# A hybrid encoder step on one core: the later tokens' last output column tile by tile, and their norm turned before it is scaled

## The chip, the cores and the metric

The kernel runs on one core of a Trainium2 chip. The metric is the device time of one execution in microseconds (us). Engine names in rows: PE is TensorE (PEld its weight loads), DVE is VectorE, ACT ScalarE, POOL GpSimd, SP SyncE; a q behind a name is that engine's issuing of DMAs.

## What is computed

One layer for 512 prompt tokens and 128 sample tokens (8 sequences of 16), 2048 wide, all float32. Cut to what matters:

```
m = silu(c) @ w_ada + b_ada;  sh1, sc1, g1, sh2, sc2, g2 = split(m, 6)     # one row per sequence
h = rmsnorm(x, norm1_g) * (1 + sc1) + sh1
z = h @ w_in        # GLU value, GLU gate, q, k, v
y_conv = silu(layernorm(causal_dwconv(za * sigmoid(zg))));  o = band_attention(q, k, v)
x = x + g1 * (concat(y_conv, o) @ w_out)
h2 = rmsnorm(x, norm2_g) * (1 + sc2) + sh2
q = h2 @ w_pq;  s = q . sub_keys;  top 16 x top 16 -> top 16 of 16384 experts, for each of 8 heads
out = sum_e softmax(s)_e * gelu(h2 . u_e) * v_e
x = x + g2 * out;  y = rmsnorm(x, final_g)
```

The prompt tokens share one conditioning row, so their scale and shift are the same for every token; the sample's differ by sequence.

## The kernel before

Tokens lie in five tiles of 128 rows: tiles 0 to 3 are the prompt's, tile 4 is the sample's. The kernel takes tiles 0 and 1 (the first tokens, `TX` = 2) through projections, attention, output projection, norm and key queries, and then tiles 2, 3 and 4 (the later tokens, `TY` = 3) through the same. While TensorE is at the later tokens, VectorE already works on the first tokens' experts.

**Expert steps.** One `step(n)` is one expert of one token tile: POOL gathers 128 rows of `u_experts` (1 MB) into one of `NU` = 4 buffers (line 695), and VectorE multiplies them with h2 and sums (line 2009). There are 5 x 8 x 16 = 640. POOL gathers at most four steps ahead. Between steps VectorE makes the choice of the next heads' experts (`choose`). The order of VectorE's work is written out by hand: `steps(k)` puts k expert steps at a place.

**The scatter and the dense passes.** For tiles 0 to 3 the value side is dense: after step 272 (`TX * P + AHEAD`) VectorE, ScalarE and POOL make one-hot rows (`burst(0)`), TensorE scatters the weights of tiles 0 and 1 into W (line 1212), and then multiplies W with all 128 blocks of 128 rows of `v_experts` (1 MB each, line 1223). After step 512 VectorE drains the eight banks (line 1939), and the same follows for tiles 2 and 3. The sample's value side is gathered row by row at the end (line 2121). W takes the place of all that lies in RB. So ScalarE's `keep_W(0)` waits until h2 and the key scores of the later tokens are stored to DRAM (`s_h2s`, `s_Ss`, lines 1553 and 1554).

**The stretch of the change.** The later tokens' output projection has four column blocks j of 512. `w_out` comes in four quarters of 1 MB (four of the 16 row blocks each), each with one buffer that is free again when the block's three tiles have used it (`w_used`, for the fourth quarter `o_done`). The loop is block, quarter, tile (lines 1157 to 1168); a quarter of a tile is four float32 matmuls of 512 columns, each two instructions in the trace. The twelve results are numbered v = 3 j + t. VectorE multiplies each with the gate and adds it to x1 (lines 2092 and 2093, `o_free`), with `steps(4)` behind each of v = 0 to 8, then 2, 1, 1 steps behind v = 9 to 11. Beside v = 10 and 11 and behind them comes `norm_tile` for tiles 2, 3 and 4: `row_scales` (sum of the four partial sums, square root on ScalarE, reciprocal, one refinement), then x1 = x1 * r * A2 + B2 in two passes of 2048. `A2` is (1 + sc2) * norm2_g, `B2` is sh2, spread over 128 partitions; for the sample both have 16 equal rows for each sequence. The sample's B2 is loaded in eight pieces into the buffer of the prompt's gate rows, which is free after v = 10. ScalarE makes the sums of squares of a tile after its last column (`row_squares`, into banks 4 to 7), and stores the last column of x1 to DRAM. TensorE turns each h2 tile with 16 transposes into four banks (`turn_h2`), ScalarE copies them out (`keep_h2T`), and then TensorE makes key queries in 16 column blocks (lines 1177 to 1190), between them the key scores.

SP issues in this order: last `w_out` block (line 453), x1 columns 0 to 1535 of each tile after v = 6, 7, 8 (line 528), the first `w_pq` block (line 453), the sample's B2 (line 534), h2 of each tile (line 537), the other `w_pq` blocks, and at the end the key scores (lines 545 and 547).

## Time and profile before

| | us |
|---|---|
| median of 3 runs | 4024.66 |
| lowest and highest | 4020.64, 4044.64 |
| the profiled execution's own time | 4015.18 |
| its span | 4013.4 |

The rows that follow are of the profiled execution. Its own time is 1.8 us more than its span, and 9.5 us below the median of the runs. Times are counted from the start of the span. A busy time is that of the engine alone; what stands in brackets behind a row is how long the engine stood idle before it, and what ended that.

### The profile page before, as it was taken

To read this page: it belongs to the slowest core of one execution; us is meant where nothing else is said; L and a number is where in the kernel's file an instruction comes from. 1 tells how busy PE (TensorE), PEld (TensorE's weight loads), DVE (VectorE), ACT (ScalarE), POOL (GpSimd) and SP (SyncE) were. 2 spreads that over 40 slices of the span, in tenths; PEclk is the share of its full clock that TensorE was granted. 3 is DMA by queue.
4 is the path that set the end of the run, shared out by engine and by line. 5 is a ranking of instruction groups with operands and counts; after the bars stand their busy time and mean duration, and the time that the engine had idled before them with its cause. 6 is when DMAs were issued, how large, how long until landed. Compare 5 with 4: busy or idle time off the path is not lost.

```text
span 4013.4 us, 33736 instructions
## 1 busy us (share of the span) xinstructions
PE 3568.6 (89%) x11903; PEld 1887.8 (47%) x11903; DVE 2743.8 (68%) x4847; ACT 450.0 (11%) x1066; POOL 1211.2 (30%) x1052
## 2 busy tenths in 40 slices
PE   4899998997994989797889999999688999997992
PEld 1566544475542754465534444444363444443441
DVE  1258843158788968879876667776897676655577
ACT  2100004010000530103400000000070000000000
POOL 1000001116423535446542222222473222222233
PEclk8999999998996789898999999999899999998996
DMA  9877753569999999997499999999919999999997
GB/s 369 272 237 256 256 184 124 174 213 405 411 415 411 376 352 385 376 409 300 186 417 421 421 414 412 421 419 418 383 71 420 421 421 421 421 421 391 421 417 307
DMA packets 344751, 1401.89 MB, mean 349 GB/s; under 512 B 22832, under 2 KB 146952, under 8 KB 203237
## 3 DMA queue, kind: packets, MB, share of 16 engines
q0 software_dynamic: 116784, 831.78, 51.0%
q1 hardware_dynamic: 226800, 563.12, 37.4%
q10 hardware_dynamic: 1008, 4.98, 0.3%
q8 instruction: 86, 1.41, 0.1%
q14 instruction: 73, 0.60, 0.0%
HBM read 1375.08 MB, written 31.42 MB: 350 GB/s over the span
## 4 chain that ended last, share of the span: by engine, by line
DMA 49%; PE 26%; issue 12%; DVE 10%; POOL 2%; ACT 0%; SPq 0%; DVEq 0%; POOLq 0%; ACTq 0%
DMA R<-in_u_experts,MS 36%; DMA R<-in_v_experts,MS 10%; PE bank L833 8%; PE bank L861 7%; PE bank L1048 4%; DVE R L1919 3%; DMA R<-in_w_ada 3%; POOL R L695 2%; DVE R L2121 2%; PE bank L773 1%; DVE R L2009 1%; PE bank L1055 1%; PE bank L750 1%; DVE R L1918 1%; DMA keyscore_scratch<-RB 0%
## 5 line engine op out<-in xcount | busy, mean ns | idle before, releaser
L695 POOL DMA_INDIRECT R<-in_u_experts,MS x640 | 889.3, 1390 | 1564.2 <-DVE MS L2009 1321.6
L2009 DVE CUSTOM_DVE_ANT_0 R<-R 128x2048 f32<-128x2048 f32 x368 | 844.6, 2295 | 417.8 <-DMA R<-in_u_experts,MS 406.2
L1223 PE MATMUL bank<-R,RB 128*128 128x512 f32 x2304 | 1019.2, 600 | 82.4 <-DMA R<-in_v_experts 82.4
L1223 PE MATMUL bank<-RB 128*128 128x512 f32 x1792 | 778.2, 592 | 0.0
L1223 PEld LDWEIGHTS bank<-R,RB 128*128 128x128 f32 x2304 | 440.2, 192 | 651.3 <-issue 550.8
L2009 DVE CUSTOM_DVE_ANT_0 R<-R,RB 128x2048 f32<-128x2048 f32 x272 | 622.8, 2290 | 113.5 <-DMA R<-in_u_experts,MS 112.4
L1223 PEld LDWEIGHTS bank<-RB 128*128 128x128 f32 x1792 | 340.5, 190 | 428.6 <-issue 428.6
L833 PE MATMUL bank<-RB,R 128*128 128x256 f32 (+1 forms) x1536 | 399.9, 421 | 28.4 <-DMA R<-in_w_pq 25.2
L2121 DVE SCALAR_TENSOR_TENSOR R<-R,MS 128x2048 f32<-128x2048 f32 x128 | 301.4, 2355 | 180.1 <-DMA R<-in_v_experts,MS 177.7
L833 PEld LDWEIGHTS bank<-RB,R 128*128 128x128 f32 x1536 | 294.2, 193 | 127.0 <-DMA R<-in_w_pq 25.8
L1048 PE MATMUL bank<-RB,R 128*128 128x384 f32 x1024 | 333.1, 486 | 1.2 <-ACT RB L1384 0.7
L861 PE MATMUL bank<-R,RB 128*128 128x512 f32 x640 | 276.6, 594 | 0.5 <-issue 0.5
L1055 PE MATMUL bank<-R,RB 128*128 128x512 f32 x576 | 252.9, 601 | 8.2 <-DMA R<-in_w_in 7.6
L695 POOL DMA_INDIRECT R<-in_v_experts,MS x128 | 150.3, 1174 | 357.0 <-DVE R L2121 335.2
L1048 PEld LDWEIGHTS bank<-RB,R 128*128 128x128 f32 x1024 | 193.3, 190 | 133.2 <-ACT RB L1384 1.1
L861 PEld LDWEIGHTS bank<-R,RB 128*128 128x128 f32 x640 | 121.5, 191 | 151.8 <-issue 151.8
L1055 PEld LDWEIGHTS bank<-R,RB 128*128 128x128 f32 x576 | 110.7, 193 | 149.0 <-issue 137.9
L1683 DVE SCALAR_TENSOR_TENSOR RB<-RB,MS 128x512 f32<-128x512 f32 x240 | 175.9, 733 | 0.0
L1212 PE MATMUL bank<-R 128*128 128x128 f32 x1024 | 145.5, 295 | 31.4 <-DVE R L1919 19.9
L1919 DVE TENSOR_SCALAR R<-MS 128x128 f32<-128x128 f32 x512 | 150.6, 353 | 9.0 <-PE bank L1212 9.0
L1212 PEld LDWEIGHTS bank<-R 128*128 128x128 f32 x1024 | 129.0, 199 | 48.4 <-DVE R L1919 37.7
L750 PE MATMUL bank<-MS,RB 128*128 128x128 f32 (+5 forms) x497 | 75.6, 301 | 74.1 <-DMA RB<-in_rel_bias_table 16.6
(317 smaller groups left out, 2178.6 us busy)
## 6 DMA issues: line engine op xcount, KB each, us to landing
R<-in_v_experts SPq DMA_DIRECT2D x144, 1024.0 KB, 9.1
RB<-in_v_experts SPq DMA_DIRECT2D x112, 1024.0 KB, 9.1
R<-in_w_ada SPq DMA_DIRECT2D x48, 2048.0 KB, 13.4
R<-in_w_in SPq DMA_DIRECT2D x20, 2048.0 KB, 18.3
R<-in_w_in SPq DMA_DIRECT2D x24, 1024.0 KB, 25.9
R<-in_w_out SPq DMA_DIRECT2D x8, 2048.0 KB, 8.0
R<-in_w_pq SPq DMA_DIRECT2D x8, 2048.0 KB, 10.4
R<-in_w_out SPq DMA_DIRECT2D x16, 1024.0 KB, 15.8
```

Source lines behind the costliest of these rows:

```text
L695: pool.indirect_dma_start(dst, None, table, bass.IndirectOffsetOnAxis(ap=expert[T_ % 2][:, c:c + 1], axis=0)).then_inc(signal, 16)
L750: return pe.transpose(out, in_, ident[0:k, 0:k])
L833: m = pe.matmul(PB[2 * par + i][:, 0:src.shape[-1]], w, src[:, k], start=(k == 0), stop=(k == KT - 1))
L861: m = pe.matmul(PB[bank][:, :], src[:, 8 * half + i, t * P:(t + 1) * P], wide[:, slot, i, :], start=(half + i == 0), stop=(half + i == 8))
L1048: m = pe.matmul(PB[bank][:, 0:NY], quad[:, q, i, c * P:(c + 1) * P], src[:, 4 * q + i], start=(q + i == 0), stop=(q + i == 6))
L1055: m = pe.matmul(PB[bank][:, :], src[:, 4 * q + i, t * P:(t + 1) * P], quad[:, q, i, :], start=(q + i == 0), stop=(q + i == 6))
L1212: m = pe.matmul(PB[n % 4][:, k * P:(k + 1) * P], oneh[n % 4][:, 1, k], oneh[n % 4][:, 0, k], start=True, stop=True)
L1223: x = pe.matmul(PB[4 * h + q][:, :], W[:, i, h * P:(h + 1) * P], vring[slot][:, q * PW:(q + 1) * PW], start=(i == 0), stop=(i == NKEY - 1))
L1683: ch.mark(STT(out=oP, in0=iP, scalar=w, in1=oP, op0=ALU.mult, op1=ALU.add))
L1919: m = TS(oneh[n % 4][:, 0, k], iota_row, turned[t % 2][:, 0, c:c + 1], turned[t % 2][:, 2, c:c + 1], ALU.is_equal, ALU.mult)
L2009: V.tensor_tensor_reduce(u, u, x, 1.0, 0.0, ALU.mult, ALU.add, dots[t % 2][:, h * TOPK + s:h * TOPK + s + 1]).then_inc(dots_done, 1)
L2121: STT(out=acc, in0=pick_rows[p % NPICK], scalar=weight[TP][:, p:p + 1], in1=acc, op0=ALU.mult, op1=ALU.add).then_inc(v_used, 1)
```

## The change

It is made in the later tokens' stretch, and has these parts:

- The sample tile comes first in each column block (`YORDER` = sample, tile 2, tile 3), for TensorE, VectorE, ScalarE and the stores.
- In the last column block TensorE takes the four quarters of one tile, then those of the next, in place of each quarter for all three.
- The sample's B2 has the sample's own gate rows as its buffer, free after v = 9, and SP issues it ahead of the first `w_pq` block.
- ScalarE squares every result as it is added (`later_square`), into two banks and two places of RB that nothing else uses then, instead of four per tile at the end.
- Only the sample tile is normed as before the turn. The two prompt tiles are scaled by their row scale alone (`xnY`: tile 2 in place, once its x1 is stored, tile 3 into the buffer of the prompt's gate rows), turned, and get A2 and B2 as per-partition scale and bias on the way out of PSUM: tile 2 on ScalarE, tile 3 on VectorE, 16 instructions of 128 columns each. `abY` holds these two, copied once by VectorE ahead of the first tokens' choices.
- The row-wise h2 of the two prompt tiles, needed for the expert steps and the store, is made behind that.
- VectorE's order: v = 9, two steps, v = 10, wait for all of B2, sample norm, row scales and copy of tile 2, v = 11, row scales and copy of tile 3, one step, the copies out of PSUM, h2 of tiles 2 and 3, the other steps. `step` waits for all of h2 before expert step 256.

```diff
--- before.py
+++ after.py
@@ -150,12 +150,16 @@
...
         xnX = [n2X, g1X]
+        YORDER = (TY - 1, *range(TY - 1))
+        abY = RB[:, 32768:32768 + 2 * KT].rearrange("p (o k) -> p o k", o=2)
...
         A2Y = [rb(KB + (2 + i) * D, D) for i in range(2)]
-        B2Y = [rb(KB + 4 * D, D), rb(KB, D)]
+        B2Y = [rb(KB + 4 * D, D), g1Y[1]]
+        xnY = [x1[TX], g1Y[0]]
+        squares = [PB[6][:, :], PB[7][:, :], rb(30720, PW), rb(30720 + PW, PW)]
@@ -523,18 +527,18 @@
...
             def x1_out(j, cols):
-                for t in range(TX, T):
-                    sp.wait_ge(o_free, 4 + 8 + 3 * j + t - TX + 1)
-                    sp.dma_start(x1_d[t][:, cols], x1[t][:, cols]).then_inc(s_x1t[t], 16)
+                for i, y in enumerate(YORDER):
+                    sp.wait_ge(o_free, 4 + 8 + 3 * j + i + 1)
+                    sp.dma_start(x1_d[TX + y][:, cols], x1[TX + y][:, cols]).then_inc(s_x1t[TX + y], 16)
...
             x1_out(2, slice(0, 3 * PW))
-            load_block(10, "w_pq", 0)
-            sp.wait_ge(o_free, 4 + 8 + 11)
+            sp.wait_ge(o_free, 4 + 8 + 10)
...
                 sp.dma_start(B2Y[1][NS * b:NS * b + NS], rows(mod_d, [[0, NS]], D, (1 + b) * 6 * D + 3 * D)).then_inc(s_sh2, 16)
-            for t in range(TX, T):
-                sp.wait_ge(s_h2, t + 1)
-                sp.dma_start(h2_d[t], x1[t]).then_inc(s_h2s, 16)
+            load_block(10, "w_pq", 0)
+            for i, y in enumerate(YORDER):
+                sp.wait_ge(s_h2, TX + i + 1)
+                sp.dma_start(h2_d[TX + y], x1[TX + y]).then_inc(s_h2s, 16)
@@ -982,12 +986,11 @@
...
-            def turn_h2(t, x):
-                pe.wait_ge(s_h2, t + 1)
+            def turn_h2(x, bank):
...
                         k = 4 * q + i
-                        m = tr(PB[4 * (t % 2) + q][:, i * P:(i + 1) * P], x[:, k * P:(k + 1) * P], P)
+                        m = tr(PB[bank + q][:, i * P:(i + 1) * P], x[:, k * P:(k + 1) * P], P)
@@ -1154,26 +1157,37 @@
...
             pe.wait_ge(pv_read, 2 * NH)
-            for j in range(4):
+            def out_quarter(j, q, i):
+                v = j * TY + i
+                if q == 0 and v >= 6:
+                    pe.wait_ge(o_free, 4 + 8 + v - 5)
+                m = quarter_rows(catY, q, YORDER[i], (v + 3) % 6)
+                if q == 3:
+                    m.then_inc(o_done, 1)
+                elif i == TY - 1:
+                    m.then_inc(w_used, 1)
+
+            for j in range(3):
...
                     weights_in(q)
-                    for t in range(TY):
-                        v = j * TY + t
-                        if q == 0 and v >= 6:
-                            pe.wait_ge(o_free, 4 + 8 + v - 5)
-                        m = quarter_rows(catY, q, t, (v + 3) % 6)
-                        if q == 3:
-                            m.then_inc(o_done, 1)
-                        elif t == TY - 1:
-                            m.then_inc(w_used, 1)
+                    for i in range(TY):
+                        out_quarter(j, q, i)
+            for i in range(TY):
+                for q in range(4):
+                    if i == 0:
+                        weights_in(q)
+                    out_quarter(3, q, i)
+            pe.wait_ge(o_free, 4 + 8 + 9)
+            pe.wait_ge(s_h2, TX + 1)
+            turn_h2(x1[TP], 4)
             pe.wait_ge(o_free, 4 + 8 + 12)
-            for t in range(TX, T):
-                if t == TX + 1:
-                    pe.wait_ge(s_sq, 2 * T)
-                if t == TX + 2:
-                    pe.wait_ge(s_h2E, 4 * (TX + 1))
-                turn_h2(t, x1[t])
-            pe.wait_ge(s_h2E, 4 * T)
+            pe.wait_ge(s_xn, T + TX + 1)
+            turn_h2(xnY[0], 0)
+            pe.wait_ge(s_xn, T + TX + 2)
+            pe.wait_ge(s_h2E, 4 * (TX + 1))
+            turn_h2(xnY[1], 4)
+            pe.wait_ge(s_h2E, 4 * (TX + 2))
+            pe.wait_ge(xT_dve, KT + KT // 2 + 4)
@@ -1368,21 +1382,33 @@
...
-            def row_squares(t, x, ready):
-                act.wait_ge(o_free, ready)
-                for c in range(4):
-                    if t >= 1:
-                        act.wait_ge(s_sq, T + t)
-                    m = A(PB[4 + c][:, :], x[:, c * 512:(c + 1) * 512], ACT.Square, accum_out=part[:, t, c:c + 1])
-                m.then_inc(s_sq, 1)
-                act.wait_ge(s_v1, t + 2)
+            def later_square(c, i):
+                t = TX + YORDER[i]
+                act.wait_ge(o_free, 4 + 8 + 3 * c + i + 1)
+                if c == 3:
+                    act.dma_start(x1_d[t][:, 3 * PW:], x1[t][:, 3 * PW:]).then_inc(s_x1t[t], 16)
+                n = TY * c + i
+                if n >= 4:
+                    act.wait_ge(s_sq, T + TX + n - 3)
+                A(squares[n % 4], x1[t][:, c * PW:(c + 1) * PW], ACT.Square, accum_out=part[:, t, c:c + 1]).then_inc(s_sq, 1)
+
+            def later_sqrt(i):
+                t = TX + YORDER[i]
+                act.wait_ge(s_v1, TX + i + 2)
...
-            def keep_h2T(t, dst, at):
+            def keep_h2T():
                 for q in range(4):
-                    act.wait_ge(s_h2T, 4 * t + q + 1)
-                    A(dst[:, 4 * q:4 * q + 4, at * P:(at + 1) * P],
-                      PB[4 * (t % 2) + q][:, :].rearrange("p (k n) -> p k n", k=4), ACT.Copy).then_inc(s_h2E, 1)
+                    act.wait_ge(s_h2T, 4 * TX + q + 1)
+                    A(h2TY[:, 4 * q:4 * q + 4, NPY:NY], PB[4 + q][:, :].rearrange("p (k n) -> p k n", k=4),
+                      ACT.Copy).then_inc(s_h2E, 1)
+                for q in range(4):
+                    act.wait_ge(s_h2T, 4 * (TX + 1) + q + 1)
+                    for i in range(4):
+                        k = 4 * q + i
+                        m = A(h2TY[:, k, 0:P], PB[q][:, i * P:(i + 1) * P], ACT.Identity,
+                              scale=abY[:, 0, k:k + 1], bias=abY[:, 1, k:k + 1])
+                    m.then_inc(s_h2E, 1)
@@ -1489,12 +1515,17 @@
...
             gelu(0)
-            for t in range(TX, T):
-                act.wait_ge(o_free, 4 + 8 + 9 + t - TX + 1)
-                act.dma_start(x1_d[t][:, 3 * PW:], x1[t][:, 3 * PW:]).then_inc(s_x1t[t], 16)
-                row_squares(t, x1[t], 4 + 8 + 9 + t - TX + 1)
-            for t in range(TX, T):
-                keep_h2T(t, h2TY, t - TX)
+            for c in range(3):
+                for i in range(TY):
+                    later_square(c, i)
+            for i in range(TY):
+                later_square(3, i)
+                if i == 1:
+                    later_sqrt(0)
+                if i >= 1:
+                    later_sqrt(i)
+            keep_h2T()
+            act.wait_ge(s_h2, T)
@@ -1759,21 +1790,21 @@
...
-            def row_scales(t):
+            def row_scales(t, i):
...
                 r, v, q = rs[:, t:t + 1], tmpa[:, t:t + 1], ssq[:, t:t + 1]
-                dve.wait_ge(s_sq, T + t + 1)
+                dve.wait_ge(s_sq, T + i + 1 + (3 * TY if i >= TX else 0))
...
                 dve.sem_inc(s_v1, 1)
-                dve.wait_ge(s_r1, t + 2)
+                dve.wait_ge(s_r1, i + 2)
...
-            def norm_tile(t, scale, shift):
+            def norm_tile(t, i, scale, shift):
...
                 x, r = x1[t], rs[:, t:t + 1]
-                row_scales(t)
+                row_scales(t, i)
@@ -1791,7 +1822,7 @@
...
             for t in range(TX):
-                row_scales(t)
+                row_scales(t, t)
@@ -1969,10 +2000,10 @@
...
                     TT(x1r[h], x1r[h], accd[h], ALU.add).then_inc(f_x, 1)
-                dve.wait_ge(s_sq, 2 * T + 1)
+                dve.wait_ge(s_sq, 2 * T + 3 * TY + 1)
...
                 row_out(x1r[2], 13)
-                dve.wait_ge(s_sq, 2 * T + 3)
+                dve.wait_ge(s_sq, 2 * T + 3 * TY + 3)
@@ -1987,7 +2018,7 @@
...
                 if n == TX * P:
-                    dve.wait_ge(s_h2, TX + 1)
+                    dve.wait_ge(s_h2, T)
@@ -2028,6 +2059,9 @@
...
             dve.wait_ge(s_h2E, 4 * TX)
+            ch.mark(CP(abY[:, 0], A2T))
+            ch.mark(CP(abY[:, 1], B2T))
+            ch.sync()
@@ -2086,8 +2120,9 @@
...
             for v in range(4 * TY):
-                j, t = divmod(v, TY)
-                x, g, at = x1[TX + t], g1Y[0 if TX + t < TP else 1], slice(j * PW, (j + 1) * PW)
+                j, i = divmod(v, TY)
+                t = TX + YORDER[i]
+                x, g, at = x1[t], g1Y[0 if t < TP else 1], slice(j * PW, (j + 1) * PW)
@@ -2098,15 +2133,31 @@
...
                     steps(4)
-                elif v == 3 * TY:
+                elif i == 0:
                     steps(2)
+                elif i == 1:
                     dve.wait_ge(s_A2, 3)
-                    dve.wait_ge(s_sh2, 16)
-                elif v < 4 * TY:
-                    norm_tile(TX + v - 3 * TY - 1, A2Y[0], B2Y[0])
-                    steps(1)
-            dve.wait_ge(s_sh2, 16 * (1 + NB))
-            norm_tile(TP, A2Y[1], B2Y[1])
+                    dve.wait_ge(s_sh2, 16 * (1 + NB))
+                    norm_tile(TP, TX, A2Y[1], B2Y[1])
+                if j == 3 and i >= 1:
+                    row_scales(t, TX + i)
+                    if i == 1:
+                        dve.wait_ge(s_x1t[t], 32)
+                    ch.mark(TS(xnY[i - 1], x, rs[:, t:t + 1], None, ALU.mult))
+                    ch.sync()
+                    dve.sem_inc(s_xn, 1)
+            steps(1)
+            for q in range(4):
+                dve.wait_ge(s_h2T, 4 * (TX + 2) + q + 1)
+                for i in range(4):
+                    k = 4 * q + i
+                    m = TS(h2TY[:, k, P:2 * P], PB[4 + q][:, i * P:(i + 1) * P], abY[:, 0, k:k + 1], abY[:, 1, k:k + 1],
+                           ALU.mult, ALU.add)
+                m.then_inc(xT_dve, 1)
+            dve.wait_ge(s_x1t[TX + 1], 32)
+            for i in range(2):
+                ch.link(TT(x1[TX + i], xnY[i], A2Y[0], ALU.mult))
+                TT(x1[TX + i], x1[TX + i], B2Y[0], ALU.add).then_inc(s_h2, 1)
```

## Rows read from the trace of the kernel before

**Rows 1.** The page: busy time of each engine, and the span in 40 slices.
```profile
PE 3568.6 (89%) x11903; PEld 1887.8 (47%) x11903; DVE 2743.8 (68%) x4847; ACT 450.0 (11%) x1066; POOL 1211.2 (30%) x1052
...
DMA  9877753569999999997499999999919999999997
```

**Rows 2.** Windows: busy us of each engine (instructions), granted clock, DMA share, GB/s.
```profile
1600.00:1645.00 45.00, 41.79 (x98) 18.24 (x96) 39.40 (x62) 3.84 (x9) 18.74 (x13) 1.00 1.02 418
1645.00:1680.00 35.00, 10.46 (x48) 9.40 (x48) 28.79 (x47) 12.12 (x31) 4.08 (x4) 0.61 0.94 348
1680.00:1770.00 90.00, 89.92 (x306) 54.96 (x307) 67.65 (x82) 7.40 (x16) 55.69 (x28) 1.00 0.98 391
...
1975.00:2893.00 918.00, 878.43 (x2024) 385.54 (x2022) 647.13 (x1038) 6.37 (x8) 267.98 (x235) 0.98 1.01 415
```

**Rows 3.** TensorE in order of time: start us, busy us, line, operation, count, idle before.
```profile
1476.72 165.07 PE L1055 MATMUL bank<-R,RB 128*128 128x512 f32 x384 [0.63 <-ACT RB L1444]
1656.06 3.59 PE L750 MATMUL bank<-MS,RB 128*128 128x128 f32 x16 [14.27 <-DVE RB L2093]
...
1680.08 36.39 PE L1048 MATMUL bank<-RB,R 128*128 128x384 f32 x112 [0.69 <-ACT RB L1384]
```

**Rows 4.** VectorE in order of time, the first scores and then the norms.
```profile
853.76 0.49 DVE L1839 MAX8 MS<-RB 128x8 f32<-128x128 f32 x2 [11.15 <-ACT RB L1390]
...
1637.14 0.68 DVE L2092 TENSOR_TENSOR MS<-bank,RB 128x512 f32<-128x512 f32 x1
...
1645.63 0.15 DVE L1766 TENSOR_REDUCE MS<-MS 128x1 f32<-128x4 f32 x1
...
1647.27 2.35 DVE L1778 SCALAR_TENSOR_TENSOR RB<-RB,MS 128x2048 f32<-128x2048 f32 x1
...
1669.28 0.16 DVE L1766 TENSOR_REDUCE MS<-MS 128x1 f32<-128x4 f32 x1 [4.44 <-DMA RB<-mod_scratch]
...
1675.52 2.28 DVE L2009 CUSTOM_DVE_ANT_0 R<-R,RB 128x2048 f32<-128x2048 f32 x1
```

**Rows 5.** SP's queue in order of time: start us, us of issuing, line, what, count.
```profile
1478.10 3.82 SPq L510 DMA_DIRECT2D RB<-mod_scratch  x8
...
1600.62 0.37 SPq L453 DMA_DIRECT2D R<-in_w_out  x1
...
1645.74 9.50 SPq L534 DMA_DIRECT2D RB<-mod_scratch  x8
```

**Rows 6.** ScalarE in order of time, before the first scatter.
```profile
1872.88 0.49 ACT L1502 ACTIVATE MS<-bank 128x384 f32<-128x384 f32 x1 [12.37 <-PE bank L750]
1877.73 1.28 ACT L1507 ACTIVATE R<-MS 128x128 f32<-128x128 f32 x4 [4.36 <-DMA keyscore_scratch<-RB]
```

**Rows 7.** VectorE in order of time, its last expert steps before the first scatter.
```profile
1863.68 2.29 DVE L2009 CUSTOM_DVE_ANT_0 R<-R,RB 128x2048 f32<-128x2048 f32 x1 [3.54 <-DMA R<-in_u_experts,MS]
...
1867.72 2.29 DVE L2009 CUSTOM_DVE_ANT_0 R<-R,RB 128x2048 f32<-128x2048 f32 x1 [1.07 <-DMA R<-in_u_experts,MS]
```

**Rows 8.** TensorE in order of time, at the first scatter and behind the dense pass.
```profile
1871.94 0.90 PE L750 MATMUL bank<-MS,RB 128*128 128x128 f32 x3 [14.38 <-DVE RB L1906]
...
2899.32 1.54 PE L750 MATMUL bank<-MS 128*128 128x128 f32 x6 [26.20 <-DVE RB L1939]
```

**Rows 9.** DMA issues of two stretches: KB each, median us from issue to landing.
```profile
RB<-mod_scratch SPq DMA_DIRECT2D x1, 1024.0 KB, 6.5
...
R<-in_w_pq SPq DMA_DIRECT2D x4, 1024.0 KB, 25.8
...
R<-in_w_out SPq DMA_DIRECT2D x1, 1024.0 KB, 17.3
...
x_scratch<-RB ACTq DMA_DIRECT2D x3, 256.0 KB, 8.4
```

**Rows 10.** Single lines of the kernel: ns min/median/max, first and last start, forms.
```profile
L1795 DVE TENSOR_SCALAR R<-RB,MS x2: 1285/1286/1287, 823.3 to 826.4; 128x2048 f32<-128x2048 f32 x2
...
L1802 DVE TENSOR_SCALAR RB<-bank,MS x8: 539/541/545, 829.8 to 832.9; 128x256 f32<-128x256 f32 x8
```

## The prediction

> **What bounds the kernel now.** I read the page first, then the stretch that the change touches by windows, by engine in order of time, and by its queue, and last what takes the new start over. On the page TensorE is busy 89% of the span, yet from the tenth slice on the DMA row is nearly full as well, but for three places [rows 1]. The windows tell which of the two counts: from 1600 on the DMA engines are busy 94% to 102% of each window, and again through the first dense pass, at 348 to 418 GB/s [rows 2]. The reader should see that a late VectorE is not caught up cheaply there: each expert step needs a gathered row of 1 MB.
>
> The stretch itself: TensorE ends the output columns of the later tokens at 1641.8, waits 14.27 us, turns three tiles (3.59 us for the first) with waits between them, and starts the key queries at 1680.08 [rows 3]. 38.3 us go by for some 10.5 us of work, the PE busy time of the window 1645:1680 [rows 2]. The gaps come from VectorE [rows 4]: it reads the bank of v = 9 (the first tile's last column) only at 1637.14, is done with v = 10 at 1645.63, does v = 11 after the first norm, and waits 4.44 us for the sample's shift rows before the last norm. The load of those is issued from 1645.74, when v = 10 is done, and takes 9.50 us to issue; it lands at 1669.28 [rows 4, 5].
>
> Now the end of that stretch, which decides. Two chains meet at the first scatter. The TensorE chain (queries, key scores, their store to DRAM) lets ScalarE go at 1877.73, after an idle of 4.36 us that ends with the key score store [rows 6]. The VectorE chain (272 expert steps) starts its last step at 1867.72, ends it at 1870.0 [rows 7], and has the pick weights ready when TensorE begins to turn them at 1871.94 (0.90 us [rows 8]); ScalarE's copy, 0.49 us from 1872.88 [rows 6], takes it to 1873.4. So TensorE's chain is late by 4.3 us and no more. Whatever it gains beyond 4.3 us is lost to the VectorE chain, and each us by which VectorE comes later than now counts once it has used those 4.3 us.
>
> Behind that the kernel passes any shift on: the first dense pass is the window 1975:2893, 1.01 DMA share at 415 GB/s [rows 2], TensorE ends it at 2873 and waits 26.20 us for VectorE's steps and drain [rows 8]. It is a fixed number of rows at a fixed rate.
>
> **The change part by part.** All times are those of the profiled execution (span 4013.4, time 4015.18); the median of the runs is 9.5 us above it, and I add the same difference at the end.
>
> *Last column tile by tile.* A matmul row is 165.07/384 = 0.43 us, a quarter of a tile 8 of them, 3.44 us, a tile 13.8 us, a column block 41.3 us, so the last block begins at 1600.5 [rows 3]. The sample tile needs the fourth weight quarter at 1610.8. That quarter is issued at 1600.62 and lands after 17.3 us, at 1617.9 [rows 5, 9]: TensorE stands for 7.1 us. The tiles are done at 1621.4, 1635.1 and 1648.9 instead of 1635 to 1641.8. This costs nothing yet, since VectorE comes to v = 9 at 1637.14 and to v = 10 at 1644.3. Nor does it bring anything: VectorE is held by steps(4) between banks.
>
> *Query weights later.* Their first three quarters wait for the last tile's quarters, 1638.6, 1642.0 and 1645.4, the fourth for 1648.9; before, they waited for the ends of quarters of all three tiles, 1610.8, 1621.1 and 1631.5, and stood behind the x1 stores in SP's order. They landed after 25.8 us at the median [rows 9], hence by 1668 and 1675; first needed at about 1670 and 1701. Covered. The 3 MB that leave the stretch 1624 to 1637 take away some of VectorE's idle before v = 9. It is busy 39.40 of 45 us in that window [rows 2], so 13.7 us of it hold some 1.7 us of idle: that is the bound of the gain, and I take 0.
>
> *Shift rows into the sample's gate buffer.* The sample's last column is done at 1637.14 + 0.71 + 0.69 = 1638.5, and now frees the buffer, 7.2 us sooner. Eight pieces follow, ahead of the query weights in SP's order. Nothing shows this load with a clear queue, so I bound it. Low: eight pieces issued in 3.82 us and a landing of 6.5 us, as a one-piece load from the same scratch had it [rows 5, 9], together 10.3 us. High: the old load, from 1645.74 to 1669.28, 23.5 us [rows 4, 5]. The old one stood behind a 1 MB weight quarter issued at 1641.8; now only the end of an x1 store is ahead. So I go near the low end, 12 us: the rows are there at 1650.5 (1648.8 to 1662.0). **This is the wait that takes the old one's place**: before, two norms were done ahead of it; now VectorE waits for it right behind v = 10, at 1645.7, for 4.8 us, and everything sits behind it: all three tiles, v = 11, the expert steps, and through these the POOL gathers.
>
> By a rule of the Trainium skill (DMA: Bandwidth & Descriptors, section Queues, rings and completion order) each engine takes descriptors of one ring in order and goes round robin between rings. With SP's ring empty but for this load that would be half the engines' rate against the gathers: an estimate of 5 us for 1 MB, 1647.3 instead of 1650.5, and a sum 3.2 us lower.
>
> *VectorE's order from there.* Sample norm: row scales 1.64 us (1645.63 to 1647.27), then two passes, 2.35 us for the first [rows 4]: 1650.5 to 1656.8. First prompt tile: row scales and the unscaled turnable copy at 1.29 us [rows 10], 1659.9. For v = 11 1.4 us, its square on ScalarE 0.8 us (the only one of twelve that is not hidden, an estimate from the 0.49 us of a 384-wide copy [rows 6]; the others lie beside it, with ScalarE busy 3.84 of 45 us [rows 2]), scales and copy 3.0 us: 1665.1. One expert step, 1667.4. TensorE turns the sample from 1656.8, the first prompt tile from 1660.5, the second from 1665.1 to 1668.8, 3.59 to 3.7 us each. ScalarE's sixteen modulated copies of the middle tile run under the third turn. The last four VectorE copies out of PSUM are not in the trace at 128x128: a 128x256 one takes 541 ns [rows 10], half of it the least, 0.54 the most, so 1.1 to 2.2 us; I take 1.5. **Queries start at 1670.3, 9.8 us sooner.** Only then come the four passes for h2, 2.3 us each: VectorE is free at 1679.4. *Two more waits* are new there, both for the 256 KB store of a tile's last x1 column, which ScalarE issues and which lands in 8.4 us [rows 9]: tile 2 is scaled in place, store from 1645.9, landed 1654.3, asked for at 1658.5; tile 3's from 1661.4, landed 1669.8, asked for at 1670.2. The second has no slack. A landing of 11 us would cost 2.2 us; behind the wait stand only h2 and the expert steps, not TensorE.
>
> *Copies of A2 and B2* beside the first scores: VectorE idles 11.15 us there [rows 4], cost 0. h2 stores come later (1675 and 1679) and SP's next query weights stand behind them; these are wanted at 1670.3 + 10.4. Nothing.
>
> **The sum.** Before, VectorE ran free from 1675.52 [rows 4] with 212 expert steps done (124, 48 beside the heads, 36 beside v = 0 to 8, and 2 + 1 + 1); now from 1679.4 with 211 (2 + 1). That is 3.9 us plus one step at (1870.0 - 1675.5)/60 = 3.2 us: 7.1 us late. Could it catch up? Its idle in that run is time for rows, and the DMA is full (0.98 and more [rows 2]); only the four rows that lie ready help. I take no catch-up. Last step 1877.1, first scatter free at 1880.5. TensorE's chain: 1877.73 - 9.8 = 1867.9, no longer last. 1880.5 - 1877.7 = +2.8 us: 4018 for this execution, **4027 us** for the median.
>
> **Bounds.** Below: shift rows at 1648.8 (-1.7), 1.7 us less contention, some 3.7 us caught up: VectorE not late, the scatter starts 4.3 us sooner. If traffic falls well, 2 us more. Above: shift rows at 1662.0, +11.5 us; and the key score store and h2 load, 3.6 MB, 8.7 us at 415 GB/s, now lie wholly before VectorE's last step, where the rows now show 3.54 and 1.07 us paid [rows 7]: 4 us more. Together about +18 us, or 20 with the store's wait.
>
> **The rivals.** (a) *VectorE keeps its time.* The load lands soon, and the traffic freed before v = 9 pays for the extra passes. For it: the load's new place in the queue, and the 4.44 us wait that goes. Against it: 2 x 1.3 us of copies, about 5 us of PSUM copies, and one step fewer done. It gives -4.3 to 0, middle 4022 us. The Trainium skill's rule above, taken alone, lies here (-0.4 us). (b) *The shift load is as slow as before*, and the inline wait stops the gathers. It decides from 1645.7 + 4.3 = 1650.0 on if nothing else were late; at 1662.0, VectorE waits 16.3 us, four rows lie ready and the gathers stop, the DMA runs partly empty where it was 94% full. +8 to +18 us, middle 4036. (c) *The new order does nothing*: VectorE's steps, not TensorE, set when the columns are read, and both chains move by less than 1 us: 4025 us.
>
> **How the numbers follow.** Forecast (0 to +8) 0.47, (a) 0.25, (b) 0.18, (c) 0.06, something not seen 0.04. From -6 us to +17 us about the median of 4024.7, with some us for a median of few runs (those before run from 4020.64 to 4044.64): 4015 to 4042. 1% is 40 us, about what a measurement of this kernel can tell from no change; none of the cases reaches it, so faster 0.02, same 0.94, slower 0.04.
>
> **What would show it.** In the changed trace: a TensorE gap of about 7 us in the last column block; a VectorE wait on the scratch load behind v = 10, of about 5 us; queries about 10 us sooner; h2 passes behind the queries' start; the 272nd step some 7 us later; ScalarE's wait for the key score store gone, with VectorE or TensorE's pick turn in its place. The forecast is wrong if VectorE's last step before the scatter ends by 1872, or after 1886, or if the dense pass, 918 us now, changes its length.

## The result, and the profile after

The changed kernel takes 4047.31 us at the median (20 runs, lowest 4038.88), the kernel before 4029.03 us on the same chips (20 runs): a ratio of 1.0044, interval 1.0027 to 1.0060, some 18 us slower. Forecast were 4027 us and a range of 4015 to 4042, so the time lies above the range.

Executions of these kernels fall on two levels some 20 us apart, the upper with a granted clock near 0.934 instead of 0.942 over the span (the profiled execution after, 4057.8 us, is on the upper), and one of the changed kernel's 20, at 5391.69 us and a clock of 0.647, is left out of the ratio. The profiled execution after is 23 us late before it comes to the changed stretch. So I count everything from t0, the first matmul of the later tokens' output projection: 1476.72 before [rows 3], 1499.79 after. From t0, ScalarE's first one-hots for the scatter start at 401.0 before [rows 6] and at 421.7 after, and behind them 2135.7 us pass before (4013.4 - 1877.73) and 2134.3 after. The 18 us arise between t0 and the scatter.

The page after, its rows of busy time and of the DMA engines (those of before are in [rows 1]), where hardly anything shows:

```profile
PE 3600.1 (89%) x11903; PEld 1907.6 (47%) x11903; DVE 2752.2 (68%) x4867; ACT 452.1 (11%) x1074; POOL 1228.3 (30%) x1052
...
DMA  9777743459999999899299999999919999999997
```

TensorE after, in order of time:

```profile
1499.79 134.17 PE L1058 MATMUL bank<-R,RB 128*128 128x512 f32 x312 [0.63 <-ACT RB L1470]
1638.29 32.65 PE L1058 MATMUL bank<-R,RB 128*128 128x512 f32 x72 [4.33 <-DMA R<-in_w_out]
1686.57 3.65 PE L754 MATMUL bank<-MS,RB 128*128 128x128 f32 x16 [15.63 <-DVE RB L1810]
...
1695.04 2.38 PE L754 MATMUL bank<-MS,RB 128*128 128x128 f32 x16 [0.47 <-DVEq L2148]
1703.14 37.21 PE L1051 MATMUL bank<-RB,R 128*128 128x384 f32 x110 [5.73 <-issue]
...
1919.22 0.90 PE L754 MATMUL bank<-MS,RB 128*128 128x128 f32 x3 [37.14 <-DVE RB L1937]
```

The queries start at t0 + 203.35. Before, it was 1680.08 - 1476.72 = 203.36 [rows 3]: the change was to bring them forward, and they start where they did. At the end TensorE, which before waited 14.38 us for the pick weights [rows 8], waits 37.14.

VectorE after, in order of time:

```profile
1667.27 0.69 DVE L2128 TENSOR_TENSOR RB<-RB,MS 128x512 f32<-128x512 f32 x1
1680.11 0.16 DVE L1797 TENSOR_REDUCE MS<-MS 128x1 f32<-128x4 f32 x1 [12.15 <-DMA RB<-mod_scratch]
...
1695.11 2.29 DVE L2040 CUSTOM_DVE_ANT_0 R<-R,RB 128x2048 f32<-128x2048 f32 x1 [0.19 <-DVE RB L2146]
...
1697.85 5.18 DVE L2154 TENSOR_SCALAR RB<-bank,RB 128x128 f32<-128x128 f32 x16
1702.95 2.28 DVE L2159 TENSOR_TENSOR RB<-RB 128x2048 f32<-128x2048 f32 x1
...
1712.01 2.29 DVE L2040 CUSTOM_DVE_ANT_0 R<-R,RB 128x2048 f32<-128x2048 f32 x1
...
1890.17 2.29 DVE L2040 CUSTOM_DVE_ANT_0 R<-R,RB 128x2048 f32<-128x2048 f32 x1 [5.01 <-DMA R<-in_u_experts,MS]
1894.85 2.29 DVE L2040 CUSTOM_DVE_ANT_0 R<-R,RB 128x2048 f32<-128x2048 f32 x1 [1.98 <-DMA R<-in_u_experts,MS]
1899.75 2.29 DVE L2040 CUSTOM_DVE_ANT_0 R<-R,RB 128x2048 f32<-128x2048 f32 x1 [2.26 <-DMA R<-in_u_experts,MS]
...
1915.00 2.28 DVE L2040 CUSTOM_DVE_ANT_0 R<-R,RB 128x2048 f32<-128x2048 f32 x1
```

Behind v = 10 VectorE stands 12.15 us for the shift rows (4.44 before, and later [rows 4]). In the 44 us from 1667.96 to 1712.01 it takes one expert step, where the kernel before took two in 30 us. The unbroken run of expert steps starts at t0 + 212.2 with the 212th, in place of 198.8 with the 213th; the 272nd step starts at 415.2 in place of 391.0. What that does to the gathers stands in GpSimd's rows, and in SyncE's queue the issue of the shift rows:

```profile
1666.84 0.94 POOL L699 DMA_INDIRECT R<-in_u_experts,MS  x1 [2.20 <-DVE MS L2040]
1698.22 0.94 POOL L699 DMA_INDIRECT R<-in_u_experts,MS  x1 [30.44 <-DVE MS L2040]
1715.11 2.59 POOL L699 DMA_INDIRECT R<-in_u_experts,MS  x1 [15.95 <-DVE MS L2040]
```

```profile
1660.71 3.79 SPq L537 DMA_DIRECT2D RB<-mod_scratch  x8
1664.54 17.80 SPq L457 DMA_DIRECT2D R<-in_w_pq  x4
```

Windows after (busy us of the engines, clock, DMA share, GB/s): the 20 us behind that issue, then t0 + 180 to 200 and 200 to 220. Of the kernel before: the same two, and t0 + 220 to 240.

```profile
1660.71:1680.71 20.00, 10.23 (x24) 4.18 (x22) 7.27 (x16) 2.90 (x6) 1.92 (x3) 0.87 1.00 267
...
1679.79:1699.79 20.00, 9.70 (x48) 8.69 (x48) 16.51 (x40) 8.46 (x25) 0.94 (x1) 0.60 0.82 314
1699.79:1719.79 20.00, 16.65 (x47) 9.83 (x48) 19.93 (x29) 0.53 (x2) 4.38 (x2) 0.91 0.58 211
```

```profile
1656.72:1676.72 20.00, 7.12 (x36) 6.46 (x35) 14.78 (x21) 6.79 (x17) 0.94 (x1) 0.67 0.93 323
1676.72:1696.72 20.00, 19.31 (x65) 12.16 (x64) 19.77 (x33) 2.39 (x4) 16.27 (x7) 0.92 0.86 329
1696.72:1716.72 20.00, 20.00 (x66) 11.92 (x65) 13.76 (x19) 0.71 (x2) 10.02 (x6) 1.00 0.98 392
```

Two different losses: first the DMA engines are shown full but move only 267 GB/s, then they stand 0.42 idle because the gathers have no free buffer. Together they are the hole from t0 + 161 to 220 in which most of the time goes: behind it the 213th step is 16.0 us later than before, and the 264th 17.7. The last eight steps add the other 6.5 us, beside the key score store and the load of h2.

And ScalarE at the scatter: it no longer waits for the key score store but for VectorE.

```profile
1921.50 1.28 ACT L1538 ACTIVATE R<-MS 128x128 f32<-128x128 f32 x4 [0.85 <-DVE R L1950]
```

### The profile page after: what moved, and what is told of

It reads as the page before. It is cut to its first block, busy times and chain, and to the rows that moved or that the text cites. A ratio compares the mean times of both kernels' runs of the same rounds, so it can differ in the third digit from the quotient of the medians.

```text
span 4055.8 us, 33767 instructions
## 1 busy us (share of the span) xinstructions
PE 3600.1 (89%) x11903; PEld 1907.6 (47%) x11903; DVE 2752.2 (68%) x4867; ACT 452.1 (11%) x1074; POOL 1228.3 (30%) x1052
## 4 chain that ended last, share of the span: by engine, by line
DMA 50%; PE 22%; issue 14%; DVE 10%; POOL 3%; ACT 0%; SPq 0%; DVEq 0%; POOLq 0%; ACTq 0%
DMA R<-in_u_experts,MS 38%; DMA R<-in_v_experts,MS 9%; PE bank L837 8%; PE bank L865 7%; DVE R L1950 3%; POOL R L699 3%; DMA R<-in_w_ada 3%; DVE R L2172 2%; PE bank L777 1%; DVE R L2040 1%; PE bank L754 1%; PE bank L1058 1%; DVE R L1949 1%; PE bank L1113 1%; PE bank L976 0%
## 5 line engine op out<-in xcount | busy, mean ns | idle before, releaser
L699 POOL DMA_INDIRECT R<-in_u_experts,MS x640 | 903.5, 1412 | 1577.6 <-DVE MS L2040 1334.6
L837 PE MATMUL bank<-RB,R 128*128 128x256 f32 (+1 forms) x1536 | 401.8, 423 | 28.9 <-DMA R<-in_w_pq 25.7
L1058 PE MATMUL bank<-R,RB 128*128 128x512 f32 x576 | 251.6, 599 | 10.7 <-DMA R<-in_w_in 5.8
L1226 PE MATMUL bank<-R 128*128 128x128 f32 x1024 | 145.0, 293 | 29.1 <-DVE R L1950 19.8
```

Source lines behind the costliest of these rows:

```text
L699: pool.indirect_dma_start(dst, None, table, bass.IndirectOffsetOnAxis(ap=expert[T_ % 2][:, c:c + 1], axis=0)).then_inc(signal, 16)
L837: m = pe.matmul(PB[2 * par + i][:, 0:src.shape[-1]], w, src[:, k], start=(k == 0), stop=(k == KT - 1))
L1058: m = pe.matmul(PB[bank][:, :], src[:, 4 * q + i, t * P:(t + 1) * P], quad[:, q, i, :], start=(q + i == 0), stop=(q + i == 6))
L1226: m = pe.matmul(PB[n % 4][:, k * P:(k + 1) * P], oneh[n % 4][:, 1, k], oneh[n % 4][:, 0, k], start=True, stop=True)
```

## The experiments

Each was timed in five rounds beside the kernel before. Times in us from t0, of its one profiled execution. "Lower" is the median time of the executions with a granted clock of 0.938 or more, less that of before in the same rounds (after: of those below the gap in its times at 4050 us). At the 208th step, ahead of most of the edits, the runs whose code is the same up to there lie within 2.7 us of each other, so a difference of less than 3 us between two rows says nothing.

| run | queries | 272nd step | one-hots | ratio [interval] | lower |
|---|---|---|---|---|---|
| before | 203.4 | 391.0 | 401.0 | 1 | 0 |
| after | 203.4 | 415.2 | 421.7 | 1.0044 [1.0027, 1.0060] | +23.6 |
| e1 | 204.2 | 415.9 | 422.4 | 1.0032 [1.0011, 1.0053] | +14.9 |
| e2 | 206.7 | 389.2 | 407.1 | 1.0002 [0.9982, 1.0022] | +0.2 |
| e3 | 205.1 | 405.8 | 412.2 | 1.0009 [0.9990, 1.0029] | +5.8 |
| e4 | 202.3 | 413.6 | 420.1 | 1.0038 [1.0019, 1.0058] | +17.3 |
| e5 | 213.0 | 425.1 | 431.6 | 1.0056 [1.0035, 1.0077] | +23.7 |
| e6 | 207.7 | 420.3 | 426.8 | 1.0045 [1.0023, 1.0067] | +17.9 |
| e7 | 217.0 | 395.7 | 415.7 | 1.0029 [1.0008, 1.0050] | +9.7 |
| e8 | 202.9 | 416.3 | 422.8 | 1.0036 [1.0015, 1.0057] | +18.0 |
| e9 | 195.8 | 404.9 | 411.4 | 1.0042 [1.0016, 1.0067] | +10.3 (3 runs) |
| e10 | 210.1 | 409.8 | 416.2 | 1.0010 [0.9992, 1.0028] | +11.1 |
| e11 | 200.7 | 399.5 | 406.0 | 1.0019 [0.9995, 1.0042] | +6.6 |
| e12 | 208.5 | 397.8 | 409.1 | 1.0011 [0.9989, 1.0032] | +4.7 |
| e13 | 210.7 | 422.6 | 429.1 | 1.0062 [1.0038, 1.0086] | +19.8 |
| e14 | 210.6 | 424.0 | 430.4 | 1.0062 [1.0041, 1.0082] | +23.7 |
| e15 | 218.2 | 399.5 | 420.0 | 1.0034 [1.0013, 1.0056] | +13.7 |

The one-hots' lateness goes with the time: in the fifteen experiments "lower" is 8 us less to 2 us more than it, 4 to 5 us less at the mean. Only three of e9's ten runs are in its last column (before: 18 of 27), so its ratio does not compare like with like and the last column rests on little. None is faster than the kernel before.

Where the steps lose their time can be told apart. For some of the runs: the 264th step, the issue of the h2 load (which goes just ahead of the key score stores), what VectorE waits for rows in its last eight steps, 265 to 272, and the 272nd step.

| run | 264th step | h2 load issued | waits, 265 to 272 | 272nd step |
|---|---|---|---|---|
| before | 365.0 | 378.2 | 4.6 | 391.0 |
| after | 382.7 | 379.6 | 11.0 | 415.2 |
| e2 | 367.0 | 383.4 | 0.8 | 389.2 |
| e3 | 374.9 | 382.1 | 9.3 | 405.8 |
| e7 | 373.7 | 393.3 | 0.9 | 395.7 |
| e9 | 373.1 | 373.3 | 10.2 | 404.9 |
| e10 | 378.0 | 387.3 | 10.4 | 409.8 |
| e11 | 368.2 | 375.5 | 9.9 | 399.5 |
| e12 | 370.2 | 385.6 | 6.2 | 397.8 |
| e15 | 377.1 | 394.4 | 1.1 | 399.5 |

The last eight steps cost 9 to 12 us of waits where the load is issued less than 10 us behind the 264th step or ahead of it (the runs that are not in this table are all of this kind, at 10.7 to 11.9 us), 4.6 and 6.2 us where it comes 13 and 15 us behind (before, e12), and about 1 us where it comes 16 us behind or later. So a part of what a run gains or loses at the 272nd step is this meeting, and not the edit's own work.

**e1 and e2: the shift rows loaded a block earlier, in the changed kernel and in the one before.**

```
-B2Y = [rb(KB + 4 * D, D), g1Y[1]]        # e2: rb(KB, D)
+B2Y = [rb(KB + 4 * D, D), rb(CX, D)]     # and the eight loads beside B2Y[0]'s, after block 8
```

> The changed kernel, with one edit: the sample's shift rows have a place of their own (the first tile's key scores are done with it) and are loaded beside the third output block, so VectorE no longer waits for them behind v = 10. All times in these expectations count from the first matmul of the later tokens' output projection (1476.72 before, 1499.79 after). There the changed kernel starts its key queries at 203.4 and turns the pick weights of the first tiles, the sign that the scatter may begin, at 419.4; the kernel before did so at 203.4 and 395.2. Theory V (VectorE's order: the wait of 12.15 us and the passes around it stop the gathers, and the scatter follows VectorE's 272nd expert step): queries at 191, 12 us sooner; the pick turn at 406 to 409, 10 to 13 us sooner; the whole kernel at 1.001 to 1.002 of before instead of 1.0044. Theory T (rival: the time is lost on TensorE's side, by the tile order of the last block and the later query weights): queries sooner at most by what the weights allow, and the pick turn stays within 3 us of 419.

> The kernel before, with the same edit alone: the sample's shift rows in a place of their own, loaded beside the third output block; the wait of 4.44 us ahead of the last norm goes. Theory V: queries 4 to 5 us sooner (199), the pick turn 0 to 4 us sooner (391 to 395), the first one-hot rows of ScalarE 3 to 5 us sooner than 401.0, the kernel at 0.998 to 1.000 of before. A theory in which only the TensorE chain counts gives the same for the queries and carries all of it to the end; one in which only the 272nd step counts gives no change of the end unless VectorE gains too.

The wait is gone in e1, and nothing is won at the one-hots (the ratios, 1.0032 and 1.0044, have intervals too wide to tell the two apart). VectorE's rows of e1, and the long waits of its stretch 1541:1661 (waits, their sum in us, times, longest):

```profile
1580.40 2.29 DVE L2040 CUSTOM_DVE_ANT_0 R<-R,RB 128x2048 f32<-128x2048 f32 x1 [4.67 <-DMA R<-in_u_experts,MS]
...
1587.01 2.29 DVE L2040 CUSTOM_DVE_ANT_0 R<-R,RB 128x2048 f32<-128x2048 f32 x1 [3.64 <-DMA R<-in_u_experts,MS]
```

```profile
DVE R L2040 <- DMA R<-in_u_experts,MS: 18.5, 18, 4.7
PE bank L1058 <- DMA R<-in_w_out: 17.6, 4, 6.5
```

In the same stretch of the changed kernel the two waits are 9.7 and 4.3 us. The load delays rows and weights where it now stands: VectorE is 8.3 us later than before at its 210th step (the changed kernel: 0.9 sooner), and most of the 12 us are paid there. e2 has the pick turn where expected (393.5) and the 272nd step 1.8 us sooner, but its queries are 3.3 us later and the key score store, waited for 12.15 us, sets the start. My expectation had the gain of the wait and no price for the place.

**e3: three expert steps into the wait.** `steps(3)` ahead of `dve.wait_ge(s_A2, 3)`.

> The changed kernel, with three expert steps put ahead of VectorE's wait for the shift rows, so that the gathers go on in it; nothing else is moved. Theory V: three steps of 2.6 to 2.9 us fit in the 12.15 us, the wait shrinks to about 4 us, the queries stay at 203.4, and the pick turn comes 8 to 10 us sooner (410), the kernel at about 1.002 of before. Theory T: the queries are where they were, so the end is where it was: 1.0044.

The 272nd step came 9.5 us sooner and the 264th 7.8 us, three steps' worth at 2.6 us; the pick turn at 409.98, as expected. So what the wait costs is the gathers' stop, not only VectorE's own time. The kernel's time, a ratio of 1.0009, no longer differs from that of before beyond its interval.

**e4: the last block in the old order**, quarter by quarter over all three tiles.

> The changed kernel, with the last output block in the old order again (each weight quarter for all three tiles); all else as changed. Theory V: VectorE comes to v = 9 later than TensorE in both orders, so nothing moves by more than 3 us: queries 203, pick turn 419, 1.004 of before; if anything slower, since the first query weights leave earlier and share the DMA engines with the gathers ahead of v = 9. Theory T: the 4.33 us in which TensorE waits for the fourth quarter and the later query weights come back, and the kernel is faster than the changed one by 5 us or more.

Nothing in the trace moves by more than 2 us, and the ratios, 1.0038 and 1.0044, do not differ beyond their intervals. That part of the change is idle: VectorE, not TensorE, sets when columns are read.

**e5, e6, e8, e13, e14: the form of the shift load.** Sixteen different rows of the stored modulation; one load of 128 partitions; rows of x_sample; four column quarters; one load from ScalarE's queue.

```
-sp.dma_start(B2Y[1][NS*b:NS*b+NS], rows(mod_d, [[0, NS]], D, (1+b)*6*D + 3*D))        # for b in range(NB)
+... rows(mod_d, [[6*D, 4], [D, 4]], D, (b % 6)*6*D + 2*D)                             # e5
+sp.dma_start(B2Y[1], rows(mod_d, [[6*D, NB], [0, NS]], D, 9*D))                       # e6; e14: act.dma_start
+... xs[NS*b:NS*b+NS]                                                                   # e8
+sp.dma_start(B2Y[1][:, q*PW:(q+1)*PW], rows(mod_d, [[6*D, NB], [0, NS]], PW, 9*D + q*PW))  # e13, q in 0..3
```

> The changed kernel, with one difference: each of the eight loads of the sample shift reads sixteen different rows of the stored modulation in place of sixteen times the same row, the same bytes and row length (so the sample rows are shifted by wrong numbers). Times below are counted from the first matmul of the later tokens' output projection. Theory S (one row read sixteen times at once by all queues is what is slow: in the changed kernel the DMA engines show 0.97 busy with only 265 GB/s in the 20 us behind the issue, against 410 GB/s with the gathers alone, and in the run with the loads set early the rate fell to some 240 GB/s for about 18 us): the loads land within 9 us of their issue, VectorE's wait of 12 us falls to 0 to 3 us, the queries start at about 194 in place of 203, the rate in those 20 us is above 350 GB/s, the 272nd step comes 8 to 14 us earlier (at 401 to 407), ratio 1.001 to 1.002. Theory B (1 MB beside full queues takes that long whatever it reads): landing 15 to 20 us after the issue, wait 10 to 13 us, 272nd step at 413 to 417, ratio 1.004.

> The changed kernel, with the eight loads of the sample shift (sixteen partitions each, all from one row) made one load of 128 partitions, so that the queues read several rows at a time; nothing is left out. Theory S (the same row read by all queues at once is slow): each row is now read by fewer queues at a time, the landing falls from 19 us to 9 to 14 us after the issue, VectorE's wait from 12 to 3 to 8 us, the 272nd step from 415 to 405 to 411 counted from the projection's first matmul. Theory B (bytes and full queues): unchanged, 12 us of wait, 415, ratio 1.004.

> The changed kernel, with the eight loads of the sample shift reading rows of the input x_sample in place of the stored modulation: the same 1 MB in rows of 8 KB, from another tensor (the sample rows are shifted by wrong numbers). Counted from the first matmul of the later tokens' output projection. Sixteen different rows of the stored modulation came no sooner than one row sixteen times, and one load of 128 partitions no sooner than eight, so two theories are left for a landing 16 to 20 us behind the issue and the fall of the DMA rate to some 240 GB/s with the engines shown busy. Theory R (reading this small stored tensor of 0.4 MB is what is slow): with the input's rows the loads land within 11 us, the rate in the 20 us behind the issue is above 340 GB/s, VectorE's wait falls to 3 to 6 us, the 272nd step comes at 404 to 410. Theory B (1 MB in such rows beside a full gather queue takes this long from anywhere): landing 15 to 22 us, wait 10 us or more, the 272nd step at 412 to 418.

> The changed kernel, with the sample shift loaded in four column quarters (128 partitions of 512 elements, 2 KB a row, as the weight quarters are, with which the DMA engines move 410 GB/s beside the gathers) in place of eight loads of 8 KB rows; nothing is left out. Without this load the 20 us around its place show 386 and 401 GB/s, with it 267 GB/s at a share of 1.00, whatever rows or tensor it reads and in eight loads or in one. Theory F (the form, 8 KB rows spread over partitions on the queue, is what is slow): the last quarter lands within 11 us of the issue, the rate in the 20 us behind the issue is above 350 GB/s, VectorE's wait falls from 12 to 6 us or less, the 272nd step comes at 403 to 409, ratio 1.001 to 1.003. Theory N (any load of this stored tensor or into these columns of SBUF is slow): landing 15 us or more, rate below 310 GB/s, 272nd step at 412 or later, ratio 1.004.

> The changed kernel, with the sample shift as one load issued by ScalarE, just ahead of its store of the sample tile's last quarter, in place of eight by SyncE ahead of the w_pq quarters; nothing is left out. Theory Q (the load is slow as it shares SyncE's queue with the 1 MB weight quarters behind it, which go round with it): landing within 12 us of its issue, VectorE's wait below 6 us, the 272nd step at 404 to 410. Rival (what is slow is the load itself, on any queue): landing 16 to 20 us, rate below 310 GB/s, wait 10 us or more, 272nd step at 412 or later; the tile's own store, now behind it on the queue, may land later still.

None of my five theories of the form brought the load sooner. From issue to the end of VectorE's wait it is 19.4 us in the changed kernel, and 27.0, 23.3, 18.8, 24.3 and 23.3 us in these five; the 20 us behind the issue show 335, 272, 288, 319 and 270 GB/s, and 267 in the changed kernel. From another queue than the weight quarters', in e14, the load is as slow.

The prediction had an estimate of 5 us from the Trainium skill (DMA: Bandwidth & Descriptors, section Queues, rings and completion order). None of these runs bears the estimate out. The rule itself, which gives turns and no durations, they do not test: what I had left out is that each transfer takes longer.

That can be read from the gathers' own DMA queue, in the 10 us from 5 to 15 us behind the issue: in the changed kernel it moves 1.27 MB in 52.3% of the 16 engines' time, without the load (e9) 2.41 MB in 57.1%. So each MB of gathered rows holds the engines 1.7 times as long beside the load. In e6, e8 and e14 it is the same (1.27 MB in 49.8%, 1.35 in 54.4%, 1.38 in 56.6%). In e5 and e13 it is 1.2 and 1.1 times (2.15 MB in 60.7%, 2.31 in 62.4%), and e15, with e13's quarters, repeats that (2.34 in 61.4%). So the form does matter for what the load takes from the others; it does not for the landing. In e5 the engines are even 0.46 idle from 20 to 25 us behind the issue (150 GB/s), and VectorE still waits for the load.

**e9: no shift load at all**, the sample tile shifted by its scale rows.

> The changed kernel without the loads of the sample shift and without VectorE's wait for them; the sample tile is shifted by its scale rows instead (wrong numbers). Theory V (the wait of 12 us and the 1 MB beside the gathers are the first cause of VectorE's lateness): the wait falls to 1 to 6 us (the store of the tile's last quarter is then what lands last), the queries start at 193 to 198 in place of 203, the 272nd step comes at 399 to 406 in place of 415, ratio 0.999 to 1.001. Rival (the wait only filled time that the gathers' buffers and the passes cost anyway): queries at 201 or later, 272nd step at 410 or later, ratio 1.003 or more.

The queries came 7.6 us sooner, the 272nd step 10.3 us, both as expected; the ratio, 1.0042, was not (0.999 to 1.001 expected). The 20 us of this run from the place at which the load would be issued:

```profile
1667.50:1687.50 20.00, 14.26 (x46) 6.91 (x44) 16.24 (x33) 3.13 (x7) 1.87 (x2) 1.00 1.00 394
```

7.9 MB in 20 us, against 5.3 MB with the load, 1.0 of them its own: the others move 3.6 MB less, 9 us of the full rate, for a transfer of 2.7 us by its bytes. Set a block earlier, in e1, the load also pulls the rate down (282 GB/s in the 20 us from 1571); in the kernel before it stood in a stretch in which the gathers were thinning out anyway (0.94, 348 GB/s [rows 2]). And the rest: without any load the 264th step is still 8.2 us later than before. That part belongs to the new order of VectorE's passes: it is about what one step fewer (3.2 us) and the copies out of PSUM (5.2 us) come to, though no run takes both away. The 272nd step is 13.9 us later, and these further 5.7 us are waits in the last eight steps.

**e7, e10, e12, e15: steps set into the turn.** e7: nine more (three in the wait, one behind the sample's passes, one behind the first unscaled pass, two ahead of the copies out of PSUM, two between the h2 passes). e10: six (three in the wait, two behind the copies, one between the h2 passes). e12: e10 with all copies on ScalarE. e15: e12 and e13 together.

> The changed kernel, with nine more of VectorE's gather steps set into the turn: three ahead of its wait for the shift rows, one behind the sample tile's two passes, one behind the first unscaled pass, two more ahead of the sixteen copies out of PSUM, two between the h2 passes. Theory V (what the change cost is the time in which no step releases a gather buffer: GpSimd's gathers stood 30.4 and 16.0 us, and the DMA engines 0.42 idle for 20 us): no stand of the gathers over 12 us, DMA share above 0.8 in every 20 us of the turn, the queries later, at 210 to 215 in place of 203, the 272nd step at 397 to 403 in place of 415, the key scores' store then the later of the two chains (one-hots at 405 to 413), ratio 0.999 to 1.002. Rival (the bytes of the last block and of the shift rows set the 272nd step, however the steps are placed): 272nd step at 406 or later, as with three steps moved, and the time no better than 1.001 and worse by the queries' delay.

> The changed kernel with three steps ahead of VectorE's wait for the shift rows, two between the sixteen copies out of PSUM and the h2 passes, one between the h2 passes: six steps more in the turn, and none of them ahead of what the queries wait for except the three that lie in the wait. Theory V: the 272nd step at 399 to 404 (three steps in the wait gave 405.8, nine gave 395.7), the queries at 203 to 207, the one-hots at 404 to 407, so a ratio of 0.999 to 1.001, the best that the changed order can be brought to. Rival (ScalarE's wait for the h2 passes ahead of its query copies holds TensorE's queries): the queries' banks come free 9 us later, the key scores' store lands 5 us or more later, the one-hots at 409 or later, ratio 1.002.

> The run with six steps more in the turn (three in the wait, two behind the copies, one between the h2 passes), with the second prompt tile's sixteen scaled copies out of PSUM made by ScalarE too, behind those of the first, so that VectorE has only its passes. Theory V (the sixteen copies are 5.2 us in which VectorE releases no gather buffer, and they stand on its chain to the 272nd step): the steps behind them start 5 us sooner, the 272nd step comes 3 to 6 us sooner than in that run (409.8), at 404 to 407; the queries start 2 to 4 us later than its 210.1, as ScalarE makes 32 copies in a row; ratio 1.000 to 1.001. Rival (the gathers' rate alone sets the 272nd step): within 2 us of 409.8, and the time 0 to 3 us worse by the queries.

> The run with six more steps in the turn and all copies on ScalarE, with the sample shift in four column quarters as well. By theory F the two gains add up: queries at 198 to 202, 272nd step at 390 to 396, one-hots at 398 to 402, and the time then no longer above that of the kernel before, ratio 0.997 to 1.000. By theory N it stays where that run was, one-hots at 409, ratio 1.001.

In e7 the 272nd step comes 19.5 us sooner, at 395.7, but only 9.0 us of that are there at the 264th, for nine steps. The other 10 us are the waits of the last eight steps, 0.9 us in place of 11.0, since its h2 load and key score stores now come behind them. GpSimd's longest stand in the turn is 10.93 us, as expected; the DMA share is 0.68 in one stretch of 20 us, not above 0.8. The price is its queries, at 217.0, and with them the key score store:

```profile
1896.49 1.28 ACT L1538 ACTIVATE R<-MS 128x128 f32<-128x128 f32 x4 [14.30 <-DMA keyscore_scratch<-RB]
```

The two chains trade: a step ahead of the queries costs TensorE's chain time, and gives VectorE's chain its own gain and, by the later stores, that of the last eight steps. e10 missed all three of its times; its steps in the wait had to wait for rows themselves (3.17 and 5.21 us), so that the sample's passes began at t0 + 187.2, 6.9 us later than in the changed kernel. e12 beats it by 12.0 us at the 272nd step, twice the 6 us that I had at most. Step by step: 4.5 us are there before the copies (its sample's passes begin at t0 + 182.7), which is how the rows fell in e10; 5.1 us come at the copies, as expected; of these 9.6 us 7.8 are left at the 264th step, and 4.2 more come with shorter waits in the last eight. At the one-hots it is the best version of the new order, and still 8.1 us late; its ratio does not stand out from those of e3 and e10. e15 met neither theory: its queries are 9.7 us later than e12's, and with them its one-hots, at 420.0.

**e11: the kernel before with the early load, and the steps between its norms moved behind the turn.** `steps(1)` behind `norm_tile(...)` left out.

> The kernel before, with the sample shift loaded early (as in the run of that name) and the three steps between its normalising passes left to stand behind the turn; nothing is left out. It tells what a step ahead of the queries is worth on each of the two chains, from the side of the kernel before. Counted from the first matmul of the later tokens' output projection. Theory V (a step there delays the queries by its own 3 us or so and gives the gathers one more release): the queries start at 197 to 200 (206.7 with the three steps), the 272nd step comes at 394 to 400 (389.2 with them), the one-hots at 399 to 403, ratio 0.998 to 1.001. Rival (the gathers set the 272nd step and make up for three steps later): 272nd step at 388 to 391, the key scores' store the later chain, one-hots at 396 to 399, ratio 0.996 to 0.999.

(The expectation speaks of three steps; the code has two there, at v = 10 and 11.) Queries 6.0 us sooner, 3.0 for each step, and the 272nd step 10.3 us later than in e2. But at the 264th it is only 1.2 us later: so far the rival, that the gathers make such steps up, has it right. The other 9 us are waits in the last eight steps, now that the key scores are ready sooner and their stores and the h2 load fall beside these rows. Three waits of e11, and e2's longest in the same steps:

```profile
1870.39 2.29 DVE L2009 CUSTOM_DVE_ANT_0 R<-R,RB 128x2048 f32<-128x2048 f32 x1 [5.66 <-DMA R<-in_u_experts,MS]
...
1875.08 2.29 DVE L2009 CUSTOM_DVE_ANT_0 R<-R,RB 128x2048 f32<-128x2048 f32 x1 [2.22 <-DMA R<-in_u_experts,MS]
...
1879.96 2.29 DVE L2009 CUSTOM_DVE_ANT_0 R<-R,RB 128x2048 f32<-128x2048 f32 x1 [1.91 <-DMA R<-in_u_experts,MS]
```

```profile
1887.19 2.30 DVE L2009 CUSTOM_DVE_ANT_0 R<-R,RB 128x2048 f32<-128x2048 f32 x1 [0.45 <-DMA R<-in_u_experts,MS]
```

So the kernel before shows it best: TensorE's chain, made shorter, brings its own traffic down on VectorE's last steps.

## Why the prediction was wrong

The direction was right (a little slower, the mechanism of the wait that takes the old one's place), and so was the frame: two chains that meet at the scatter with 4.3 us between them (3.5 by the result: 24.2 late at the step, 20.7 at the one-hots), a dense pass that passes the shift on. The size was 7 times too small at the scatter: +2.8 us forecast, +20.7 measured. The forecast's own sign of being wrong, a last step that ends after 1886 in the time of the profile before, is passed by 8 us (1894.2). VectorE's 272nd step was put 7.1 us late and is 24.2 us late. The 17.1 us between, by the prediction's own steps:

- **The shift rows' landing, the term "12 us": +6.5 us.** The issue came where it was put (t0 + 160.9; forecast 161.8). The load took 19.4 us, so that the wait ended at t0 + 180.3 and not 173.8, and was 12.15 us, not 4.8. I took the low end of my two bounds because the queue ahead was clear; the engines were full of gathers (388 GB/s in the 10 us ahead of the issue), and beside the load every transfer took longer. This is rival (b), with its point of decision (1650.0, that is t0 + 173.3) passed by 7 us; the +20.7 us lie above its +8 to +18 as well. e9 shows what the load costs by taking it away.
- **The copies out of PSUM, the term "1.5 us": +3.0 us.** I had VectorE copying beside the third turn, with only the last four behind it. It came from its expert step 2.8 us into the turn, and all sixteen took 5.18 us, 0.32 us each, within my bounds of 0.27 to 0.54. The slip was in the forecast's own times: its step ended at 1667.4 and its turn at 1668.8, which leaves 1.4 us for twelve copies. From the end of the wait to the free run it was 31.9 us, not 28.9; to the queries 23.0, not 19.8. The term and the landing together (6.5 + 3.2) are the whole 9.8 us by which the queries were to come sooner; that they start within 0.01 us of before is chance.
- **"I take no catch-up": +7.6 us.** The steps did not merely fail to catch up, they lost more: 61 steps in 205.3 us (3.37 each) against 60 in 194.5 (3.24). Most of it comes at the end: six waits from 1890.17 on add up to 10.97 us, where the two of before are 4.61 [rows 7], beside the key score store and the h2 load. The 4 us for this stood among the upper bounds. But the forecast had VectorE 7.1 us later and the key scores 9.8 us sooner; with these figures of its own all of that traffic lies before the last step, and it belonged in the sum, with 6.4 us instead of 4.

6.5 + 3.0 + 7.6 = 17.1. The range's top was made of the same pieces (11.5 + 4, with 2 for a store), but the range ended at +17 and the copies were not among them. The time is 18.3 us above that of before in the same rounds, so it would have missed a range about that median too, if by 1 us only.

Right: TensorE's stand in the last block (4.33 us, put at 7.1, and of no effect: e4); the h2 passes out of the queries' way (begun at 1702.95, the queries at 1703.14); the gate buffer freed 8 us sooner (7.2 forecast); the key score wait gone from ScalarE; the stretch behind the scatter unchanged (1.4 us shorter). The wait for a tile's store, put at the edge, shows in none of the rows. Rival (a) fell; of (c) the part that e4 undoes is true, the rest not.

**What stays open.** Why the load lands so late in every form: not the repeated row, the tensor, eight pieces or one, 8 KB rows or 2 KB, nor the queue. And why it makes the gathers' transfers longer in some forms and hardly in others: not its place in SBUF (e1 has another, with 282 GB/s), nor the tensor alone (e5 and e13 read the one of the changed kernel), nor a repeated row alone (e8 has none and is as bad, e13 has it and is not). The weight quarters, as large and read from larger tensors, leave the rate at 412 GB/s (changed kernel, the 60 us from 1559.79, six of them issued). What an expert step is worth in the turn is not one number either: by the 264th step three gained 7.8 us (e3), nine 9.0 (e7) and six 4.7 (e10).

## What to carry to other kernels

When DMA is the bound, the worth of an order of work is how long the engine that frees the gather buffers goes without freeing one: count steps per stretch, before counting its waits. A transfer has no price of its own; take it from the fullest place in which it was seen, and look at what the others move meanwhile, not at the share of busy time. When one chain's stores come just ahead of another chain's end, as here the key scores', ask on which side of its last steps they will fall: it is worth up to 10 us here, more than most of the edits. And when two chains meet, an edit that shortens one by lengthening the other's stretch is worth only the slack between them, here 4.3 us.

## What the runs showed of the hardware

- DMA engines shown at 0.99 to 1.02 moved 241 to 299 GB/s in the 20 us behind the issue of one 1 MB load beside the gathers (its form in the changed kernel: after, e3, e4, e7, e10, e12; 270 to 288 in e6, e8 and e14), 319 to 352 with it in other forms (e5, e13, e15), and 394 without it (e9). A share of 1 does not say that the engines are at their rate.
- Eight expert steps wait 9 to 12 us for their gathered rows where the 1 MB load of h2 and the key score stores are issued between 3 us ahead of their start and 9 us behind it, and about 1 us where these come 16 us or more behind it (table in the section on the experiments).
- Sixteen 128x128 copies out of PSUM with a scale and a bias take VectorE 5.18 us, ScalarE 5.73 us (VectorE's row is shown above, ScalarE's here, both of the changed kernel):

```profile
1694.59 5.73 ACT L1409 ACTIVATE RB<-bank,RB 128x128 f32<-128x128 f32 x16
```
